# A decoder step on one core: cached keys in three passes of the rounded format, values of all sequences in one accumulator

## The chip, the core and the metric

The kernel runs on one NeuronCore of a Trainium2 chip. The metric is the device time of one execution in microseconds (us). The engines are TensorE (PE, with PEld for its weight loads), VectorE (DVE), ScalarE (ACT), GpSimd (POOL) and SyncE (SP), which only issues DMAs here.

## What is computed

One inference step of a two-layer hybrid decoder, for a prompt of 256 tokens and, at the same time, for 8 sample sequences of one new token each. Each sample sequence has 2048 past tokens in 16 pages of 128, and a page holds 256 latents and 32 rotary values a token. The change is in the attention of the 8 sample sequences over these pages (all in fp32):

```python
latent = concatenate([past_latent, latent_new])                    # S x 256
k_nope = einsum('bsc,chd->bshd', latent, w_uk)                     # 4 heads x 64
v = einsum('bsc,chd->bshd', latent, w_uv)
k = concatenate([k_nope, krope for each head])                     # 96 wide
k = _rmsnorm(k, g_qk_k)                                            # over the 96
k = concatenate([k[..., :64], _rope(k[..., 64:], pos_k)])
p = softmax(q @ k * 96 ** -0.5); o = p @ v
```

Around it, per layer: projections, a gated linear attention, pooling, the prompt's own attention, cross-attention to 256 memory rows and an MLP of 4096.

## The kernel before

Every engine has one hand-written program; semaphores connect them, and each engine runs its instructions in order. SIGNALS lists the semaphores, and `Counts` counts on each engine how often one was used. There is no planner: the order of the code is the order of the queues.

Activations lie transposed (features on partitions, 264 token columns: 256 of the prompt, 8 samples). Weights stream through `ring` (4 slots of 128x2048, SP). Weight products run in three passes of the rounded fp32 format (fp32r): ScalarE copies an operand to its rounded high part, VectorE subtracts that and rounds the rest, and TensorE adds high x high, high x low and low x high (`split_product`, L1461). Other products are fp32 (`product`, L1470), which the profile shows as two records each.

**The decode stage.** After the input projection, each layer handles its 8 sequences in 8 pairs of pages each, 64 pairs. For a pair:

- SP loads the 256 latents of both pages, transposed, into `latT` (L321). The tile holds 16 pages. A pair's place is free when TensorE is done with it (`pair_ready`), so SP runs eight pairs ahead.
- TensorE (`pair`, L1717) multiplies each page with `wuq_b`, 260 columns: 256 of `w_uk`, and 4 query columns of this sequence with the key weights folded in. That gives every cached key and its raw scores, in two PSUM banks out of four. It waits for the square and the scores two pairs before (`pair_sq`, `pair_sc`).
- ScalarE squares the 256 columns (into one of three `psq`) and copies the scores (`keys`, L578).
- VectorE sums the squares by head (`pair`, L1099, the instruction at L1102), for the norm.

Between pairs each engine has its share of the prompt's attention and of the gated linear attention: `fill(b, n)`, 41 parts at places given by PLACES; VectorE takes a part one pair later than TensorE, ScalarE two. Also between pairs, the previous sequence goes on: `rotary` (TensorE, n = 0), `scores` (VectorE, n = 0), inverse root on ScalarE, `maxima` (n = 1), a reduction over the partitions on GpSimd (L425), `exponents` (n = 2), the exponentials on ScalarE (n = 3, into `pr`), `sums` (VectorE, n = 4), and `values` (n = 5). `values` on TensorE (L1729) waits for `dec_sum`, and multiplies the 16 pages of `lat` (loaded by GpSimd, 288 values a token, L374) with `pr[:, pg, :]`, 32 columns of which four are in use, four pages at a time in the four column groups. L1738 adds the new token, L1740 the sums for the denominator. VectorE divides (L1142, L1143) into `o4`, and `latents` (L1758) adds the four groups with `sel` at the end of the next `rotary`; VectorE copies the result to `olat` (L1111).

```python
for pg in range(PAGES):
    q = 32 * (pg % 4)
    mm(t[q:q + 32, 0:256], pr[:, pg, :], lat[:, b % 2, pg, 0:256], start=pg < 4, stop=pg >= PAGES - 3)
```

During sequence 7, ScalarE and VectorE also round the memory tokens and the first weights of the stage after it. Ahead of sequence 0, VectorE prepares queries and gates (its last instruction before the first sum of squares is L953); GpSimd runs the pooling additions (L403 to L418) until about 96 us. TensorE starts pair 0 as soon as the queries of sequence 0 stand in `wuq_b` (`seq_in`).

## Time and profile before

| | us |
|---|---|
| median of 3 timed runs (lowest, highest) | 1282.72 (1279.86, 1284.19) |
| the profiled execution | 1277.03 |
| its span | 1275.4 |
| busy: TensorE, VectorE, ScalarE, GpSimd | 1220.0, 804.4, 509.6, 200.6 |
| mean granted TensorE clock | 0.983 |
| DMA | 250.42 MB, 196 GB/s |

Times in the trace are counted from the start of the span. An engine's busy time is a share of the whole span, over stages with different limits. In a row of groups, the busy time of the group is followed by the mean duration of one instruction in ns; matmuls follow each other sooner than they last, since they are pipelined. In a timeline a row merges like instructions that follow each other, and brackets give the idle time before and what ended it.

### The profile page before, as it was taken

To read this page: it belongs to the slowest core of one execution; us is meant where nothing else is said; L and a number is where in the kernel's file an instruction comes from. 1 tells how busy PE (TensorE), PEld (TensorE's weight loads), DVE (VectorE), ACT (ScalarE), POOL (GpSimd) and SP (SyncE) were. 2 spreads that over 40 slices of the span, in tenths; PEclk is the share of its full clock that TensorE was granted. 3 is DMA by queue.
4 is the path that set the end of the run, shared out by engine and by line. 5 is a ranking of instruction groups with operands and counts; after the bars stand their busy time and mean duration, and the time that the engine had idled before them with its cause. 6 is when DMAs were issued, how large, how long until landed. Compare 5 with 4: busy or idle time off the path is not lost.

```text
span 1275.4 us, 24330 instructions
## 1 busy us (share of the span) xinstructions
PE 1220.0 (96%) x9392; PEld 1101.0 (86%) x9392; DVE 804.4 (63%) x1372; ACT 509.6 (40%) x908; POOL 200.6 (16%) x343
## 2 busy tenths in 40 slices
PE   4999999989999899999999999999899999999998
PEld 4987867779988799999999777677799968999998
DVE  5568675767674776655456857646767567766442
ACT  4232322443443456543442324232443425656331
POOL 1243442220000000000012723224100000000000
PEclk9999999998999999999999999999999999999999
DMA  8615665572459744545475556447446794554552
GB/s 336 247 51 167 193 187 159 171 262 100 165 219 382 281 176 168 194 172 189 173 254 199 147 165 200 141 141 233 173 157 231 293 380 154 177 187 171 193 174 92
DMA packets 76626, 250.42 MB, mean 196 GB/s; under 512 B 11440, under 2 KB 46592, under 8 KB 55904
## 3 DMA queue, kind: packets, MB, share of 16 engines
q1 hardware_dynamic: 60976, 196.14, 43.5%
q0 software_dynamic: 13424, 45.47, 10.8%
q10 hardware_dynamic: 2112, 7.26, 1.4%
q8 instruction: 75, 1.23, 0.4%
q14 instruction: 39, 0.32, 0.1%
HBM read 241.60 MB, written 7.46 MB: 195 GB/s over the span
## 4 chain that ended last, share of the span: by engine, by line
PE 79%; DVE 7%; DMA 5%; issue 4%; ACT 2%; PEld 1%; POOLq 0%; POOL 0%; DVEq 0%; ACTq 0%; PEldq 0%
PE ps L1461 50%; PE ps L1470 19%; PE ps L1737 2%; DMA ring<-in_units 2%; DMA big<-in_pages 2%; DVE ring_r L766 1%; PE ps L1897 1%; PEld ps L1461 1%; DVE ssn L1102 1%; DVE xg_r L782 1%; DMA xT<-in_xt 1%; PE ps L1696 1%; PE ps L1697 1%; ACT big_r L454 1%; DVE rB L789 1%
## 5 line engine op out<-in xcount | busy, mean ns | idle before, releaser
L1461 PE MATMUL ps<-qkA_r,ring_r 128*128 128x264 f32 x880 | 251.9, 286 | 0.0
L1470 PE MATMUL ps<-wuq_b,latT 128*128 128x260 f32 x1024 | 249.6, 395 | 0.9 <-ACT sc L454 0.9
L1470 PEld LDWEIGHTS ps<-wuq_b,latT 128*128 128x128 f32 x1024 | 193.6, 194 | 40.8 <-issue 9.2
L374 POOL DMA_DIRECT2D big<-in_pages x256 | 138.9, 543 | 226.8 <-DVEq L730 196.8
L1461 PEld LDWEIGHTS ps<-qkA_r,ring_r 128*128 128x128 f32 x880 | 168.0, 191 | 0.0
L1461 PE MATMUL ps<-big_r,ring_r 128*128 128x264 f32 x512 | 145.5, 284 | 0.0
L766 DVE TENSOR_TENSOR ring_r<-ring,latT_r 128x2048 fp32r<-128x2048 f32 x42 | 96.3, 2292 | 61.2 <-ACT latT_r L454 60.3
L454 ACT ACTIVATE latT_r<-ring 128x2048 fp32r<-128x2048 f32 x42 | 80.4, 1915 | 111.7 <-DMA ring<-in_units 111.7
L454 ACT ACTIVATE qkA<-ps 128x512 f32<-128x512 f32 x86 | 51.1, 594 | 173.7 <-PE ps L1470 163.7
L1461 PE MATMUL ps<-xg_r,latT_r 128*128 128x264 f32 (+1 forms) x384 | 110.5, 288 | 0.0
L1461 PE MATMUL ps<-qkA_r,latT_r 128*128 128x264 f32 x320 | 94.4, 295 | 15.4 <-DVE xg_r L782 15.1
L1102 DVE TENSOR_REDUCE ssn<-qkA 128x8 f32<-128x512 f32 x86 | 59.0, 686 | 73.5 <-ACT qkA L454 69.3
L1461 PE MATMUL ps<-area_r,latT_r 128*128 128x264 f32 (+1 forms) x352 | 100.3, 285 | 0.0
L1461 PEld LDWEIGHTS ps<-big_r,ring_r 128*128 128x128 f32 x512 | 96.2, 188 | 0.0
L766 DVE TENSOR_TENSOR ring_r<-ring,big_r 128x2048 fp32r<-128x2048 f32 x28 | 67.5, 2410 | 15.2 <-ACT big_r L454 13.4
L1461 PEld LDWEIGHTS ps<-qkA_r,latT_r 128*128 128x128 f32 x320 | 61.8, 193 | 16.7 <-DVE ring_r L766 14.3
L1461 PEld LDWEIGHTS ps<-xg_r,latT_r 128*128 128x128 f32 x384 | 73.9, 192 | 0.4 <-issue 0.2
L1461 PE MATMUL ps<-qkB_r,ring_r 128*128 128x264 f32 x256 | 72.9, 285 | 0.0
L1461 PE MATMUL ps<-big_r,latT_r 128*128 128x264 f32 x256 | 72.3, 282 | 0.0
L454 ACT ACTIVATE big_r<-ring 128x2048 fp32r<-128x2048 f32 x28 | 53.1, 1910 | 47.9 <-DMA ring<-in_units 47.9
L1461 PEld LDWEIGHTS ps<-area_r,latT_r 128*128 128x128 f32 x352 | 66.2, 188 | 0.1
L766 DVE TENSOR_TENSOR ring_r<-ring,sq_r 128x2048 fp32r<-128x2048 f32 x20 | 45.8, 2291 | 31.9 <-ACT sq_r L454 31.6
(372 smaller groups left out, 2919.2 us busy)
## 6 DMA issues: line engine op xcount, KB each, us to landing
ring<-in_units SPq DMA_DIRECT2D x136, 1024.0 KB, 4.9
big<-in_pages POOLq DMA_DIRECT2D x256, 144.0 KB, 3.4
latT<-in_pages SPq DMA_DIRECT2D x256, 128.0 KB, 2.7
big<-in_units SPq DMA_DIRECT2D x12, 1024.0 KB, 10.5
mat<-in_mats POOLq DMA_DIRECT2D x2, 2048.0 KB, 11.3
mat<-in_units SPq DMA_DIRECT2D x4, 1024.0 KB, 8.4
xg<-in_memt SPq DMA_DIRECT2D x2, 1024.0 KB, 5.8
out_mk<-latT ACTq DMA_DIRECT2D x2, 1024.0 KB, 3.9
```

Of the source, the lines that this page charges most:

```text
L374: pool.dma_start(lat[:, s, pg, :], pages[bass.ds(at_page[pg] * DEPTH + l, 1), :, 256:544] .rearrange("a p n -> p (a n)")).then_inc(lat_in[ ...
L454: return nc.scalar.activation(out, in_, func, **kw)
L766: v.tensor_tensor(ring_r[:, s, :], ring[:, s, :], his[s].bitcast(FP32), ALU.subtract).then_inc(sems["unit_lo"], 1)
L782: v.scalar_tensor_tensor(xg_r[:, k, :], xT[:, k, :], gain[:, g + k:g + k + 1], hi_x[:, k, :].bitcast(FP32), ALU.mult, ALU.subtract).then_i ...
L789: step(v.tensor_tensor(rB[:, :], x_sqs[0] if k == 1 else rB[:, :], x_sqs[k % 4], ALU.add))
L1102: v.tensor_reduce(ssn[:, s, 2 * n:2 * n + 2, :], psq[(at["pair_sq"].n - 1) % 3].rearrange("p (g c) -> p g c", c=64), AXX, ALU.add).then_in ...
L1461: ins = mm(out, a(i, k), b(j, k), start=first and k + n == 0, stop=last and k == KD - 1 and n == 2)
L1470: ins = mm(out, a, b, start=i == 0, stop=i == len(pairs) - 1)
L1696: mm(t[:, c0:c0 + keys_to], normed[n_rows, i, q0:q0 + P], normed[n_rows, 4 + i, 0:keys_to], start=True, stop=False)
L1697: ins = mm(t[:, c0:c0 + keys_to], normed[r_rows, 2, q0:q0 + P], normed[r_rows, 3, 0:keys_to], start=False, stop=True)
L1737: mm(t[q:q + 32, 0:256], pr[:, pg, :], lat[:, b % 2, pg, 0:256], start=pg < 4, stop=pg >= PAGES - 3)
L1897: ins = mm(t[32 * h:32 * h + 32, 0:NM], hot[:, c, b * H + h, :], u[:, h, c, :], start=b + c == 0, stop=b + c == B)
```

## The change

**Keys.** `latT` becomes five slots of raw pairs (`raw_of`, pages 0 to 9) and three slots of high parts (`high_of`, pages 10 to 15). ScalarE writes the high part of pair n + 3 right behind the square and the scores of pair n (`key_high`); VectorE writes the low part over the raw page right behind the sum of pair n (`key_low`). Both do pairs 0 to 2 ahead of the loop. The weights and queries in `wuq_r` have both parts too. TensorE waits for `key_lo` instead of the page and runs six rounded products a page in place of two in fp32. For odd sequences the query columns stand behind the weights, for even ones ahead of them, so the weights are stored once. SP can run five pairs ahead.

**Values.** `pr` becomes 60 columns wide with one sequence's probabilities in the middle. Each sequence takes another window of 32 columns of it, so its four columns fall on other output rows, and VectorE adds the results of all sequences in one `o4` (copy, six additions, one addition with the division). The new tokens (`p_new`), the denominators and `sel` (now 32 columns) come once, with the last sequence. `values` on TensorE waits for `dec_exp` instead of `dec_sum`.

The diff, without declarations and calls that only pass a sequence's number:

```diff
@@ -24,2 +24,4 @@
 S_PAGES = PAGES + 1
+PR0 = (B - 1) * H
+WIDE_PR = PR0 + B * H
 NM = 256
...
@@ -110,2 +112,14 @@
+RAW, HIGH = 5, 3
+PAIRS = B * PAGES // 2
+def raw_of(q):
+    return slice(2 * (q % RAW), 2 * (q % RAW) + 2)
+def high_of(q):
+    return slice(2 * (RAW + q % HIGH), 2 * (RAW + q % HIGH) + 2)
 POOL_STEPS = 20
@@ -147,3 +161,2 @@
 big, big_r = twin("big", [P, 2 * PAGES * 288])
-krQ = sb("krQ", [P, PAGES, ROPE])
 krN = sb("krN", [P, PAGES, ROPE])
@@ -152,3 +165,3 @@
 rBm = sb("rBm", [P, NM + 2])
-wuq_b = sb("wuq_b", [P, 2, 2, 260])
+_, wuq_r = twin("wuq", [P, 2, 2, 264])
 qt = sb("qt", [P, 2, B, H])
@@ -161,8 +174,9 @@
 scw = sb("scw", [P, S_PAGES, H])
-pr = sb("pr", [P, S_PAGES, 32])
+pr = sb("pr", [P, PAGES, WIDE_PR])
 mxp = sb("mxp", [P, H])
 mx = sb("mx", [P, H])
-rs = sb("rs", [P, 32])
+p_new = sb("p_new", [P, B * H])
+rs = sb("rs", [P, B * H])
 den = sb("den", [P, 1])
-sel = sb("sel", [P, H])
+sel = sb("sel", [P, B * H])
 olat = sb("olat", [P, 2, B, H])
@@ -209,3 +223,4 @@
-o4 = within(qkB_f, 1024, 2, 256)
+o4 = within(qkB_f, 1024, 256)
+krQ = within(qkA_f, 1216, PAGES, ROPE)
 ssm = tmp[:, 512:512 + NM]
...
@@ -317,2 +332,3 @@
             for pg in range(PAGES):
+                q = l * PAIRS + (b * PAGES + pg) // 2
                 src = pages[bass.ds(at_page[pg] * DEPTH + l, 1), :, :].rearrange("a p n -> p (a n)")
@@ -320,3 +336,3 @@
                     sp.wait_ge(sems["pair_ready"], at["pair_ready"].free())
-                sp.dma_start(latT[:, pg, :], src[:, 0:256]).then_inc(lt_in[pg // 4], 16)
+                sp.dma_start(latT[:, raw_of(q).start + pg % 2, :], src[:, 0:256]).then_inc(lt_in[q % RAW], 16)
                 if b == B - 1 and pg == 7:
...
@@ -577,4 +592,12 @@
+        def key_high(n):
+            if n < PAIRS:
+                q = l * PAIRS + n
+                act.wait_ge(lt_in[q % RAW], 32 * (q // RAW + 1))
+                f(latT_r[:, high_of(q), :], latT[:, raw_of(q), :], ACT.Copy).then_inc(sems["key_hi"], 1)
         def keys(b, mem=False):
+            sums, scores = (slice(4, 260), slice(0, 4)) if b % 2 == 0 else (slice(0, 256), slice(256, 260))
             for pair in range(PAGES // 2):
@@ -583,5 +606,6 @@
                 q = pair % 2
-                f(psq[(at["pair_sum"].n - 1) % 3].rearrange("p (g c) -> p g c", g=2), ps[:, 4 + 2 * q:6 + 2 * q, 0:256],
+                f(psq[(at["pair_sum"].n - 1) % 3].rearrange("p (g c) -> p g c", g=2), ps[:, 4 + 2 * q:6 + 2 * q, sums],
                   ACT.Square).then_inc(sems["pair_sq"], 1)
-                f(sc[:, b % 2, 2 * pair:2 * pair + 2, :], ps[:, 4 + 2 * q:6 + 2 * q, 256:260], ACT.Copy).then_inc(sems["pair_sc"], 1)
+                f(sc[:, b % 2, 2 * pair:2 * pair + 2, :], ps[:, 4 + 2 * q:6 + 2 * q, scores], ACT.Copy).then_inc(sems["pair_sc"], 1)
+                key_high(b * (PAGES // 2) + pair + HIGH)
                 if b and pair == 1:
...
@@ -618,6 +642,9 @@
-        def exp():
+        def exp(b):
             act.wait_ge(sems["dec_in"], at["dec_in"].next())
-            f(pr[:, :, 0:H], scw[:, :, :], ACT.Exp, scale=QK ** -0.5).then_inc(sems["dec_exp"], 1)
+            f(p_new[:, H * b:H * b + H], scw[:, PAGES, :], ACT.Exp, scale=QK ** -0.5)
+            f(pr[:, :, PR0:PR0 + H], scw[:, 0:PAGES, :], ACT.Exp, scale=QK ** -0.5).then_inc(sems["dec_exp"], 1)
+        for n in range(HIGH):
+            key_high(n)
         for b in range(B):
...
@@ -857,3 +884,5 @@
-            step(v.tensor_copy(wuq_b[:, b % 2, :, 256:260], qt[:, :, b, :]))
+            c = 0 if b % 2 == 0 else 260
+            step(v.tensor_copy(wuq_r[:, 0, :, c:c + 4], qt[:, :, b, :]))
+            step(v.tensor_tensor(wuq_r[:, 1, :, c:c + 4], qt[:, :, b, :], wuq_r[:, 0, :, c:c + 4].bitcast(FP32), ALU.subtract))
             tell("seq_in")
...
@@ -888,4 +917,4 @@
                 dve.wait_ge(layer_in, 64 * (l + 1))
-                for s in range(2):
-                    step(v.tensor_copy(wuq_b[:, s, :, 0:256], w_uk))
+                step(v.tensor_copy(wuq_r[:, 0, :, 4:260], w_uk))
+                step(v.tensor_tensor(wuq_r[:, 1, :, 4:260], w_uk, wuq_r[:, 0, :, 4:260].bitcast(FP32), ALU.subtract))
                 step(v.tensor_copy(s_raw[NOPE:QK, 1, :].rearrange("p (h b) -> p h b", b=B),
@@ -1098,2 +1127,10 @@
+        def key_low(n):
+            if n < PAIRS:
+                q = l * PAIRS + n
+                wait("key_hi")
+                v.tensor_tensor(latT_r[:, raw_of(q), :], latT[:, raw_of(q), :], latT_r[:, high_of(q), :].bitcast(FP32),
+                                ALU.subtract).then_inc(sems["key_lo"], 1)
         def pair(s, n):
@@ -1109,4 +1146,2 @@
             t = tile()
-            if b:
-                step(v.tensor_copy(olat[:, :, b - 1, :], t[:, 64:72].rearrange("p (c h) -> p c h", c=2)))
             mean, rows = of_decode[1], ssn[:, b % 2, :, :]
@@ -1133,5 +1168,5 @@
-        def sums():
+        def sums(b):
             wait("dec_exp")
-            step(v.tensor_reduce(rs[:, 0:H], pr[:, :, 0:H].rearrange("p g h -> p h g"), AXX, ALU.add))
+            step(v.tensor_reduce(rs[:, H * b:H * b + H], pr[:, :, PR0:PR0 + H].rearrange("p g h -> p h g"), AXX, ALU.add))
             tell("dec_sum")
@@ -1141,4 +1176,10 @@
             t = tile()
-            step(v.reciprocal(den[:, :], t[:, 256:257]))
-            freed(v.tensor_scalar(o4[:, b % 2, :], t[:, 0:256], den[:, :], None, ALU.mult))
+            if b == 0:
+                freed(v.tensor_copy(o4, t[:, 0:256]))
+            elif b < B - 1:
+                freed(v.tensor_tensor(o4, o4, t[:, 0:256], ALU.add))
+            else:
+                step(v.reciprocal(den[:, :], t[:, 256:257]))
+                freed(v.tensor_tensor(o4, o4, t[:, 0:256], ALU.add))
+                step(v.tensor_scalar(o4, o4, den[:, :], None, ALU.mult))
             tell("lat_used")
@@ -1157,2 +1198,3 @@
                 pair(s, n)
+                key_low(b * (PAGES // 2) + n + HIGH)
                 if n == 1 and b:
...
@@ -1199,2 +1241,4 @@
         last = B - 1
+        for n in range(HIGH):
+            key_low(n)
         for b in range(B):
...
@@ -1223,3 +1267,3 @@
         mem_keys(2)
-        freed(v.tensor_copy(olat[:, :, last, :], tile()[:, 0:8].rearrange("p (c h) -> p c h", c=2)))
+        freed(v.tensor_copy(olat[:, :, :, :], tile()[:, 0:2 * B * H].rearrange("p (c b h) -> p c b h", c=2, b=B)))
         tell("olat_ready")
@@ -1500,3 +1544,3 @@
     pe.sem_inc(sems["unit_used"], SLOTS)
-    pe.sem_inc(sems["pair_ready"], PAGES // 2)
+    pe.sem_inc(sems["pair_ready"], RAW)
     for l in range(DEPTH):
@@ -1721,7 +1765,10 @@
             pe.wait_ge(sems["pair_sc"], at["pair_sc"].free())
-            if n % 2 == 0:
-                pe.wait_ge(lt_in[n // 2], 64 * (l * B + b + 1))
-            for pg in (2 * n, 2 * n + 1):
-                ins = product(ps[:, 4 + 2 * q + pg % 2, 0:260],
-                              [(latT[:, pg, P * c:P * c + P], wuq_b[:, b % 2, c, :]) for c in range(2)])
+            wait("key_lo")
+            at_pair = l * PAIRS + b * (PAGES // 2) + n
+            w0 = 4 * (b % 2)
+            for a in range(2):
+                hi, lo = (latT_r[:, of(at_pair).start + a, :] for of in (high_of, raw_of))
+                ins = product(ps[:, 4 + 2 * q + a, 0:260],
+                              [(x[:, P * c:P * c + P], wuq_r[:, j, c, w0:w0 + 260]) for c in range(2)
+                               for x, j in ((hi, 0), (hi, 1), (lo, 0))])
             ins.then_inc(sems["pair_ready"], 1)
@@ -1730,3 +1777,3 @@
-            wait("dec_sum")
+            wait("dec_exp")
             pe.wait_ge(lat_in[b % 2], 16 * PAGES * (l * (B // 2) + b // 2 + 1))
@@ -1736,6 +1783,11 @@
                 q = 32 * (pg % 4)
-                mm(t[q:q + 32, 0:256], pr[:, pg, :], lat[:, b % 2, pg, 0:256], start=pg < 4, stop=pg >= PAGES - 3)
-            mm(t[0:32, 0:256], pr[:, PAGES, :], latn[:, :], start=False, stop=True)
-            for q in range(0, P, 32):
-                ins = mm(t[q:q + 32, 256:257], rs[:, :], ones[:, 0:1], start=True, stop=True)
+                ins = mm(t[q:q + 32, 0:256], pr[:, pg, PR0 - H * b:PR0 - H * b + B * H], lat[:, b % 2, pg, 0:256],
+                         start=pg < 4, stop=pg >= PAGES - 4 + (b == B - 1))
+            if b == B - 1:
+                mm(t[0:32, 0:256], p_new[0:B, :], latn[0:B, :], start=False, stop=True)
+                pe.wait_ge(sems["dec_sum"], B * (l + 1))
+                for q in range(0, P, 32):
+                    mm(t[q:q + 32, 256:257], rs[:, :], ones[:, 0:1], start=True, stop=False)
+                    ins = mm(t[q:q + 32, 256:257], p_new[0:B, :], ones[0:B, 0:1], start=False, stop=True)
             ready(ins)
@@ -1749,11 +1801,9 @@
                 ins = product(t[:, 16 * g:16 * g + 16], [(krC[:, g, :], qbs[:, b % 2, 0:16]), (krS[:, g, :], qbs[:, b % 2, 16:32])])
-            if b:
-                ins = latents(t, 64, b - 1)
             ready(ins)
-        def latents(t, o, b):
+        def latents(t):
-            wait("lat_used")
+            pe.wait_ge(sems["lat_used"], at["lat_used"].next(B))
             for c in range(2):
-                ins = mm(t[:, o + H * c:o + H * c + H], o4[:, b % 2, P * c:P * c + P], sel[:, :], start=True, stop=True)
+                ins = mm(t[:, B * H * c:B * H * c + B * H], o4[:, P * c:P * c + P], sel[:, :], start=True, stop=True)
             return ins
...
```

VectorE's queue at the start of the stage, before the change. `ssn` is the sum of squares, `area<-ps` (L984) belongs to a fill part:

```order
L951 TENSOR_TENSOR sq<-area,sq 128x256 [waits gate_exp,tile_free]
L952 SCALAR_TENSOR_TENSOR sq<-area,sq 128x256 [waits dve_step]
L953 TENSOR_TENSOR sq<-area,sq 128x256 [waits dve_step]
L1102 TENSOR_REDUCE ssn<-qkA 128x8 [waits dve_step,pair_sq]
L1102 TENSOR_REDUCE ssn<-qkA 128x8 [waits pair_sq]
L984 TENSOR_SCALAR area<-ps 128x256 [waits tile_ready]
```

The same place in the changed kernel:

```order
L980 TENSOR_TENSOR sq<-area,sq 128x256 [waits gate_exp,tile_free]
L981 SCALAR_TENSOR_TENSOR sq<-area,sq 128x256 [waits dve_step]
L982 TENSOR_TENSOR sq<-area,sq 128x256 [waits dve_step]
L1133 TENSOR_TENSOR latT_r<-latT,latT_r 128x512 [waits dve_step,key_hi]
L1133 TENSOR_TENSOR latT_r<-latT,latT_r 128x512 [waits key_hi] x2
L1139 TENSOR_REDUCE ssn<-qkA 128x8 [waits pair_sq]
L1133 TENSOR_TENSOR latT_r<-latT,latT_r 128x512 [waits key_hi]
L1139 TENSOR_REDUCE ssn<-qkA 128x8 [waits pair_sq]
L1133 TENSOR_TENSOR latT_r<-latT,latT_r 128x512 [waits key_hi]
L1013 TENSOR_SCALAR area<-ps 128x256 [waits tile_ready]
```

Three low parts stand behind the preparation and ahead of the first sum, and one more behind each sum.

TensorE's queue in sequence 1, pairs 0 and 1, before the change (the second and fourth rows of products are fill parts):

```order
L1470 MATMUL ps<-wuq_b,latT 128x260 [waits pair_sc,pair_sq]
L1470 MATMUL ps<-wuq_b,latT 128x260 x3
L1627 MATMUL ps<-area,mat 64x256 [waits tile_free,lat_ready]
L1627 MATMUL ps<-area,mat 64x256 x11
L1470 MATMUL ps<-wuq_b,latT 128x260 [waits lt_in1,pair_sc,pair_sq]
L1470 MATMUL ps<-wuq_b,latT 128x260 x3
L1648 MATMUL ps<-area,mat 32x256 [waits tile_free]
```

And now:

```order
L1514 MATMUL ps<-wuq_r,latT_r 128x260 [waits key_lo,pair_sc,pair_sq]
L1514 MATMUL ps<-wuq_r,latT_r 128x260 x11
L1671 MATMUL ps<-area,mat 64x256 [waits tile_free,lat_ready]
L1671 MATMUL ps<-area,mat 64x256 x11
L1514 MATMUL ps<-wuq_r,latT_r 128x260 [waits key_lo,pair_sc,pair_sq]
L1514 MATMUL ps<-wuq_r,latT_r 128x260 x11
L1692 MATMUL ps<-area,mat 32x256 [waits tile_free]
```

Twelve products stand for four, and every pair waits for VectorE's low part.

## Rows read from the trace of the kernel before

**Rows 1.** The page, part 1: busy us (share of the span) xinstructions by engine.
```profile
PE 1220.0 (96%) x9392; PEld 1101.0 (86%) x9392; DVE 804.4 (63%) x1372; ACT 509.6 (40%) x908; POOL 200.6 (16%) x343
```

**Rows 2.** The page, part 5: the cached keys' products on TensorE, two records a product.
```profile
L1470 PE MATMUL ps<-wuq_b,latT 128*128 128x260 f32 x1024 | 249.6, 395 | 0.9 <-ACT sc L454 0.9
```

**Rows 3.** Busy us by stretch: PE, PEld, DVE, ACT, POOL, PEclk, DMA share, GB/s.
```profile
85.20:96.27 11.07, 11.07 (x59) 9.02 (x58) 8.38 (x14) 7.15 (x18) 9.19 (x11) 1.00 0.36 97
96.27:107.48 11.21, 11.21 (x56) 8.54 (x55) 10.42 (x18) 2.00 (x6) 8.18 (x15) 1.00 0.81 233
107.48:265.25 157.77, 152.39 (x1023) 117.66 (x1022) 101.37 (x225) 49.45 (x149) 50.92 (x96) 0.98 0.59 179
265.25:294.29 29.04, 23.94 (x159) 20.55 (x159) 21.41 (x47) 15.73 (x35) 4.32 (x9) 0.91 0.49 191
```

**Rows 4.** Who waited, 107 to 265: us in total, times, longest; VectorE and TensorE.
```profile
DVE ssn L1102 <- ACT qkA L454: 26.3, 18, 2.9
...
DVE ssn L1102 <- ACT qkB L454: 11.9, 8, 5.3
...
DVE scw L1131 <- POOL mx L425: 4.3, 2, 3.4
...
PE ps L1737 <- DVEq L730: 3.8, 3, 1.9
```

**Rows 5.** Timeline, TensorE: start us, us, engine, line, operation, count; four pairs without fills.
```profile
266.57 7.26 PE L1470 MATMUL ps<-wuq_b,latT 128*128 128x260 f32 x32
```

**Rows 6.** Busy us by stretch: rounded products without a gap, columns as Rows 3.
```profile
500.00:525.00 25.00, 25.00 (x207) 25.00 (x206) 16.89 (x23) 13.58 (x20) 0.00 (x0) 1.00 0.53 190
```

**Rows 7.** Groups of instructions, TensorE: busy us, mean ns, idle before.
```profile
L1738 PE MATMUL ps<-latn,pr 128*32 128x256 f32 x32 | 10.4, 411 | 0.0
...
L1758 PE MATMUL ps<-sel,qkB 128*128 128x4 f32 x64 | 9.2, 250 | 0.0
```

**Rows 8.** Groups of instructions on VectorE and ScalarE, same columns.
```profile
L1069 DVE TENSOR_TENSOR ring<-ring 128x512 f32<-128x512 f32 x2 | 1.4, 692 | 0.1
...
L858 DVE COPY wuq_b<-qt 128x8 f32<-128x8 f32 x16 | 2.7, 172 | 2.1
...
L454 ACT ACTIVATE krN<-big 128x512 f32<-128x512 f32 x16 | 10.0, 626 | 9.2 <-DMA big<-in_pages 9.2
```

**Rows 9.** Timeline, VectorE: two instructions without a wait between them.
```profile
206.81 0.69 DVE L1102 TENSOR_REDUCE ssn<-qkB 128x8 f32<-128x512 f32 x1
207.41 0.68 DVE L1195 TENSOR_REDUCE ssr<-krQ 128x16 f32<-128x512 f32 x1
```

**Rows 10.** Timelines of the stage's start: TensorE, VectorE, GpSimd.
```profile
78.42 3.18 PE L1470 MATMUL ps<-wuq_b,latT 128*128 128x260 f32 x8
81.44 2.32 PE L1470 MATMUL ps<-xg,ones 128*128 128x256 f32 x10
...
82.41 0.43 DVE L951 TENSOR_TENSOR sq<-area,sq 128x256 f32<-128x256 f32 x1
82.87 1.62 DVE L952 SCALAR_TENSOR_TENSOR sq<-area,sq 128x256 f32<-128x256 f32 x1
84.53 0.52 DVE L953 TENSOR_TENSOR sq<-area,sq 128x256 f32<-128x256 f32 x1
...
82.59 1.62 POOL L403 TENSOR_TENSOR area<-ue 128x798 f32<-128x798 f32 x1 [0.53 <-POOL ue L401]
...
87.36 0.69 DVE L1102 TENSOR_REDUCE ssn<-qkA 128x8 f32<-128x512 f32 x1 [1.47 <-ACT qkA L454]
...
93.11 3.12 DVE L993 TENSOR_SCALAR qsb<-area,con 128x8 f32<-128x8 f32 x4
```

**Rows 11.** Timeline, GpSimd: the first reduction over the partitions in layer 0.
```profile
118.85 0.39 POOL L425 PARTITION_ALL_REDUCE mx<-mxp  x1 [10.71 <-issue]
```

**Rows 12.** The page, part 6: pages of keys, KB each, median us to landing.
```profile
latT<-in_pages SPq DMA_DIRECT2D x256, 128.0 KB, 2.7
```

**Rows 13.** Busy us by stretch, columns as Rows 3: TensorE mostly idle.
```profile
276.00:280.00 4.00, 1.76 (x16) 1.02 (x18) 1.75 (x5) 3.16 (x8) 0.00 (x0) 1.00 0.99 414
```

19 lines of the change are left out of this document (9 added, 10 removed).

## The prediction

> **What bounds the kernel now.** I read the page's shares first: TensorE is busy for 96% of the span, VectorE for 63% [rows 1]. The costliest line but one is the product of the cached keys: 1024 records, 249.6 us, with 0.9 us of waiting before them [rows 2]. Then the busy times by stretch. In layer 0 the decode stage goes from VectorE's first sum of squares at 85.20 to its last at 294.29, 209.1 us. In sequences 1 to 6 (107.48 to 265.25) TensorE is busy for 152.4 of 157.8 us, VectorE for 101.4 [rows 3]. What VectorE waits for there is ScalarE's squares, 26.3 + 11.9 us [rows 4], and these come from TensorE's products. So TensorE sets the pace of the stage, and VectorE has a third of it free. No instruction outside this stage is edited to speak of, and layer 1 has the same program as layer 0: I work out one layer and double it.
>
> **What TensorE saves.** Four pairs with nothing between them took 7.26 us: 1.8 us a pair [rows 5]. Products in the rounded format run at 25 us / 207 = 0.121 us each for 264 columns at the full clock [rows 6]; a pair now has 12 of them, 1.45 us. That is 0.35 x 128 = 45 us. L1738, the new token's latents, goes in 14 of 16 sequences at 10.4 / 16 = 0.65 us, L1758 falls from 64 records to 4, 9.2 us to 0.6 [rows 7]: 9 + 9 us. Together 63 us, if TensorE kept the pace. It does not.
>
> **What VectorE gets.** Each of 64 pairs a layer adds one TENSOR_TENSOR of 128x512, 0.69 us [rows 8]. No wait for its own step stands behind it, and an instruction after such a one starts 0.60 us later (206.81, 207.41) [rows 9]; I take 0.60. Where an instruction does wait for the step before, 0.035 us pass in between (82.41 + 0.43, next at 82.87) [rows 10]. The other edits on VectorE (a small one more for the queries, a reciprocal and a copy gone, an addition for a multiplication) cancel: nothing. So per layer [rows 3]:
> - Sequences 1 to 6: 101.4 busy, 225 gaps x 0.035 = 7.9, 48 x 0.60 = 28.8: 138.1 us, where 157.8 passed: **-19.7**. TensorE's own work there is 152.4 - 48 x 0.35 - 6 x 1.2 = 128: VectorE is the bound now.
> - Sequence 7: 21.4 + 1.6 + 5 x 0.60 = 26.0, where 29.0 passed: **-3.0**.
> - Sequence 0 from pair 4 on: 10.4 + 0.6 + 4 x 0.60 = 13.4, where 11.2 passed: **+2.2**. VectorE sets the pace there already.
>
> ScalarE gets one copy of 128x512 a pair, 0.63 us by the copy to krN [rows 8]: 40 us beside its 67 in these three stretches of 198 us. It stands right behind the square and the scores of the same pair, while VectorE sums that square for 0.69 us. I count nothing.
>
> **The start of the stage.** TensorE began pair 0 at 78.42, beside VectorE's preparation, whose last instruction (L953) ended at 85.05. Now pair 0 waits for key_low(0), which stands behind that preparation in VectorE's queue and is reached at about 85.6. GpSimd's additions run there (busy for 9.2 of the next 11.1 us, [rows 3]): in the shadow of one, from 82.59, VectorE's L952 took 1.62 us, where L951 of the same size took 0.43 [rows 10]. Held as long, key_low(0) ends at 87.4. TensorE has idled for nearly 9 us by then and comes back at the half clock, as it ran pair 0 in the trace, 3.18 us for eight records: 2.9 us for 12 rounded products at twice 0.121. Then fill part 0 (2.3 us at full clock, I take 2.6), pair 1 and ScalarE's square: VectorE sums pair 1 at 95.0, not at 87.36. Its work from there to pair 4 was 8.4 - 0.7 = 7.7 us busy; with gaps and three key_lows 10.0. But the four instructions L993, 3.12 us for 128x8, ran beside GpSimd and would come after it now, where 128x8 takes some 0.2 (L858): -2.2 [rows 8, 10]. Pair 4 is reached at 102.8 instead of 96.27: **+6.5**. Bounds: +4 (nothing held, full clock), +9 (no -2.2).
>
> **The waits that stay.** Where VectorE is the bound, each wait of its own is paid. One is sure: the first reduction over the partitions in a layer comes late, with 10.7 us on GpSimd that nothing in the view explains, and VectorE waited 3.4 us for it [rows 4, 11]. A key_low now stands ahead of it: 2.8. For the rest there are two ends. From 96.27 to 107.48, where VectorE sets the pace, 0.2 of 11.2 us was waiting, 2%; over all of sequence 0 it was 22.3 less 18.8 and 1.1 of gaps, 11%. On the 164 us above that is 3.3 or 18 us; I take 7.7, nearer the first, because TensorE may run three pairs ahead and has over 30 us to spare. This is to cover the heavy fills, pages that land late, and the later reductions, which stand behind sixteen page loads in GpSimd's queue. In all **+10.5**.
>
> Five slots for raw pairs instead of eight cost nothing in the forecast: a slot comes free about two pairs (6 us) before ScalarE wants its next content, and a page lands after 2.7 us [rows 12]. Without that cover each pair would cost up to a microsecond; the upper end has it.
>
> **Sum.** -19.7 - 3.0 + 2.2 + 6.5 + 10.5 = -3.5 us a layer, -7 in all: 1277.0 becomes 1270.0 for the profiled execution. The median of the timed runs is 5.7 us above that execution, so the forecast is **1275.7 us**, 0.5% faster. Under 0.3%, 3.9 us, a measurement of this kernel hardly tells from no change.
>
> **A rule against the change.** In the 4 us from 276, TensorE was busy for 1.76 and its clock was still the full one, 1.00 [rows 13]. VectorE as the bound gives TensorE gaps of half a microsecond a pair, far less idle time than that, so the sum counts its work at the full clock. The Trainium skill (TensorE: Matmul & The Clock Gate, HAM oscillation) says that waits between bursts of matmuls bring the throttle back again and again. By that rule the sum would be that of rival 2; the trace does not bear it out for such a short idle time.
>
> **Rivals.**
> 1. *VectorE keeps its waits; slower.* The place is the hand-over in sequences 1 to 6: a key_low holds VectorE's fill part behind it, and TensorE's products wait for the key_low of three pairs before. If the engines take turns instead of overlapping, VectorE keeps, say, 60% of its 42.5 us of waiting there [rows 4] and of 6 in sequence 7: 29 instead of 10.5, which is +15 a layer, +30 in all, 1313. It decides from 14 us of waits a layer, where the gain is gone; above 16 the kernel is slower by over 0.3%. For it: TensorE waited 3.8 us there for VectorE's sums of the exponents already [rows 4]. Against it: the values' product no longer waits for these.
> 2. *TensorE at the half clock for half of the stage; slower.* Its work of some 199 - 32 = 167 us a layer, less 4 for the low clock already in it, becomes 163 / 0.75 = 217, more than VectorE's. With the start at +6.5 that is 15 us a layer more than the 209 now: 1313. For it: pair 0 above ran at the lower clock after small products. Against: [rows 13].
> 3. *The waits almost vanish.* Only the reduction and the 2% stay, 6.2 us: -8 a layer, 1267; with the start at +4, 1262. For it: TensorE's reserve.
> 4. *TensorE stays the bound and all of its 63 us show*: 1220. VectorE's sum excludes it, unless the added instruction costs far less than 0.60. It would be the change as its TensorE part alone reads.
>
> **Numbers.** By waits of 7 to 14 us a layer the forecast goes from 1269 to 1283: 0.50. Rival 1, above 14 us, up to 1313: 0.26. Rival 2: 0.06. Rival 3, below 7 us: 0.16. Rival 4: 0.02. From 1259 to 1302 leaves out rivals 2 and 4, a third of rival 1 and a little of rival 3: two in ten. Faster by over 0.3% (under 1278.9, up to 12 us of waits) are rivals 3 and 4 and two thirds of the forecast: 0.52; within it 0.19; slower (over 1286.5) 0.29.
>
> **What would show it.** Right: 1.45 us a pair for the keys on TensorE; VectorE busy for over 85% in sequences 1 to 6, its waits for ScalarE's squares under 10 us there, and TensorE waiting for key_low instead; TensorE idle for 8 to 9 us before pair 0; a stage of some 206 us. Wrong: a TensorE still without gaps, a key_low that takes its place at another price than 0.60, or a VectorE busy for under 80% of the stage.

## The result and the profile after

The changed kernel took 1313.86 us (median of 4 runs, 1306.78 to 1318.06), the kernel before 1283.45 (4 runs): a ratio of 1.0235, 95% interval 1.0178 to 1.0291. It is **slower** by 30 us; the forecast was 1275.7 with a range from 1259 to 1302. The profiled execution took 1306.78 us, with a span of 1305.0; the one of before had a span of 1275.4.

The page of after, parts 1 (busy time, share, instructions) and 2 (three of its rows):

```profile
PE 1198.2 (92%) x9724; PEld 1105.5 (85%) x9724; DVE 883.3 (68%) x1490; ACT 576.6 (44%) x1052; POOL 202.8 (16%) x342
...
PE   4978989889999899999999698898699999999998
...
DVE  5569788778674677664556888978757657766432
...
PEclk8979899888999999999999799989899999999999
```

Beside [rows 1], TensorE is busy for 22 us less and VectorE for 79 us more. The two decode stages are slices 3 to 10 and 23 to 29, and there the granted clock now dips. Over the span it is 0.954, before it was 0.983.

The page, part 5, the two costliest groups of the change:

```profile
L1514 PE MATMUL ps<-wuq_r,latT_r 128*128 128x260 f32 x1536 | 227.4, 304 | 40.1 <-DVE latT_r L1133 29.9
...
L1133 DVE TENSOR_TENSOR latT_r<-latT,latT_r 128x512 fp32r<-128x512 f32 x128 | 93.1, 730 | 0.3
```

The first answers [rows 2]. The keys' products take 22 us less, not 45, and TensorE has idled 40 us before them, mostly for VectorE's split, where it idled 0.9.

The stretches of layer 0 that answer to [rows 3] (from the first sum of squares to pair 4 of sequence 0, to sequence 1, sequences 1 to 6, sequence 7), and a last row for all of them in layer 1; the columns are those of [rows 3]:

```profile
92.35:105.65 13.30, 13.30 (x96) 12.21 (x95) 10.73 (x18) 10.00 (x25) 9.94 (x14) 0.95 0.49 141
105.65:119.27 13.62, 10.62 (x73) 8.76 (x71) 12.84 (x21) 3.92 (x10) 4.10 (x8) 1.00 0.67 225
119.27:277.68 158.41, 143.34 (x1125) 118.59 (x1125) 128.96 (x269) 74.18 (x203) 48.63 (x92) 0.91 0.54 167
277.68:309.16 31.48, 26.50 (x173) 23.35 (x173) 24.01 (x50) 17.92 (x40) 6.11 (x12) 0.73 0.63 226
732.30:946.75 214.45, 185.09 (x1454) 154.53 (x1454) 173.83 (x349) 105.11 (x274) 68.30 (x124) 0.93 0.57 179
```

The stage of layer 0 ends at 309.16 and not at 294.29, 14.9 us later (its last sum of squares starts at 306.16, before at 291.25); the whole span grew by 29.6. Layer 1's last sum starts 27.5 us later than before, so nearly the whole loss lies in these stages. Sequences 1 to 6, where the forecast had its gain, take 158.4 us, as long as before. VectorE's busy time there rose from 101.4 to 129.0, and the granted clock there is 0.91 where it was 0.98.

Who waited in these sequences, 119 to 278 (us in total, times, longest), VectorE's waits and TensorE's largest:

```profile
DVE ssn L1139 <- ACT qkB L469: 7.8, 4, 4.0
...
DVE ssn L1139 <- ACT qkA L469: 6.2, 6, 1.8
PE ps L1514 <- DVE latT_r L1133: 4.9, 3, 2.8
...
DVE scw L1166 <- POOL mx L440: 2.8, 1, 2.8
```

VectorE's waits for squares fell from 38.2 us [rows 4] to 14.0, and TensorE now waits for the low halves. Both engines wait, in turn: neither is the bound of the whole stretch. Of the 29.9 us that TensorE waited for the low halves, 18.2 are the two waits ahead of pair 0, one a layer; in sequences 1 to 6 it was 4.9 in layer 0 and 3.9 in layer 1.

The start of the stage, timelines of TensorE and VectorE (start, duration, engine, line, operation; in brackets the idle time ahead):

```profile
88.75 2.94 PE L1514 MATMUL ps<-wuq_r,latT_r 128*128 128x260 f32 x12 [9.18 <-DVE latT_r L1133]
...
86.84 3.17 DVE L1133 TENSOR_TENSOR latT_r<-latT,latT_r 128x512 fp32r<-128x512 f32 x3
92.35 0.69 DVE L1139 TENSOR_REDUCE ssn<-qkA 128x8 f32<-128x512 f32 x1 [2.34 <-ACT qkA L469]
92.95 1.88 DVE L1133 TENSOR_TENSOR latT_r<-latT,latT_r 128x512 fp32r<-128x512 f32 x1
```

TensorE stands for 9.2 us before pair 0 and takes 2.94 us for its 12 products, at the level of 1.2 GHz. At 2.4 GHz, 24 of them took 3.15 us (101.42), 1.5 to 1.6 a pair. Of the splits, the first took 1.77 us, the fourth 1.88 and the fifth 1.43, while GpSimd added beside them; of 128, the mean is 0.73.

### The profile page after: what moved, and what is told of

Its sections match the earlier page's. It is cut to its first block, busy times and chain, and to the rows that moved or that the text cites. A ratio compares the mean times of both kernels' runs of the same rounds, so it can differ in the third digit from the quotient of the medians.

```text
span 1305.0 us, 25249 instructions
## 1 busy us (share of the span) xinstructions
PE 1198.2 (92%) x9724; PEld 1105.5 (85%) x9724; DVE 883.3 (68%) x1490; ACT 576.6 (44%) x1052; POOL 202.8 (16%) x342
## 4 chain that ended last, share of the span: by engine, by line
PE 64%; DVE 20%; issue 6%; DMA 4%; ACT 3%; PEld 1%; POOL 0%; POOLq 0%; DVEq 0%; ACTq 0%; PEldq 0%
PE ps L1505 49%; PE ps L1514 9%; DVE latT_r L1133 3%; DVE ssn L1139 3%; DMA ring<-in_units 2%; DMA big<-in_pages 2%; DVE ring_r L793 2%; PE ps L1947 1%; PEld ps L1505 1%; DVE xg_r L809 1%; DVE qkB L1226 1%; PE ps L1740 1%; DMA xT<-in_xt 1%; DVE qkB L1225 1%; PE ps L1741 1%
## 5 line engine op out<-in xcount | busy, mean ns | idle before, releaser
L1514 PE MATMUL ps<-wuq_r,latT_r 128*128 128x260 f32 x1536 | 227.4, 304 | 40.1 <-DVE latT_r L1133 29.9
L1514 PEld LDWEIGHTS ps<-wuq_r,latT_r 128*128 128x128 f32 x1536 | 206.6, 203 | 61.4 <-issue 46.1
L1133 DVE TENSOR_TENSOR latT_r<-latT,latT_r 128x512 fp32r<-128x512 f32 x128 | 93.1, 730 | 0.3
L469 ACT ACTIVATE latT_r<-latT 128x512 fp32r<-128x512 f32 x128 | 80.7, 634 | 1.1 <-DMA latT<-in_pages 1.1
```

What stands on the lines that cost most here:

```text
L469: return nc.scalar.activation(out, in_, func, **kw)
L1133: v.tensor_tensor(latT_r[:, raw_of(q), :], latT[:, raw_of(q), :], latT_r[:, high_of(q), :].bitcast(FP32), ALU.subtract).then_inc(sems["key ...
L1514: ins = mm(out, a, b, start=i == 0, stop=i == len(pairs) - 1)
```

## The experiments

Eleven kernels ran, each timed against the kernel before on the same chip. They ran on three chips, on which the kernel before took 1282.0, 1282.8 and 1279.2 us: where two of them differ by a few us, the ratios to it say more than the times. All end in one table, at the end of this section. The expectations speak of theories by letters; each is spelled out where it first stands.

### The two parts of the change alone

**The values' part.** The accumulator of all sequences is kept; pages, weights and products of the keys are those of before:

```diff
-                    wait("key_lo")
...
-                                       for x, j in ((hi, 0), (hi, 1), (lo, 0))])
+                    if n % 2 == 0:
+                        pe.wait_ge(lt_in[n // 2], 64 * (l * B + b + 1))
...
+                                      [(latT[:, pg, P * c:P * c + P], wuq_b[:, b % 2, c, :]) for c in range(2)])
```

Expected: 

> The values of all sequences in one accumulator, with the keys in fp32 as before. The change came out 30 us slower than before, and the question is where. Theory V (VectorE has become the bound of sequences 1 to 6 and hands over late, since the split pages gave it 128 more instructions of 0.73 us): this part takes nothing to VectorE, so it gains what TensorE saves in it, at most the 18 us of [rows 7], 1265 to 1275 us. Theory C (TensorE waits more and runs at its 1.2 GHz level after it): also faster, 1265 to 1278, and the windows at 1.2 GHz in the decode stage are as few as before. Theory A (the one accumulator itself costs, by the chain of additions into o4 or the values' wait): 1290 or more.

Measured: 1265.82 us (ratio 0.987, 0.9843 to 0.9898). This part alone is **faster by 16 us** and is the fastest kernel here that leaves nothing out of the computation.

**The keys' part.** The reverse: three rounded passes, with a sum, a division and a turn for each sequence as before.

```diff
-                    if b == 0:
-                        freed(v.tensor_copy(o4, t[:, 0:256]))
...
+                    step(v.reciprocal(den[:, :], t[:, 256:257]))
+                    freed(v.tensor_scalar(o4[:, b % 2, :], t[:, 0:256], den[:, :], None, ALU.mult))
```

Expected: 

> The keys in three rounded passes with split pages, with the values as before (a sum and a division for each sequence). Theories V and C: the whole loss lies here, so 1314 plus what the values' part saves, 1320 to 1332 us. Theory A: nearly as fast as before, 1275 to 1290 us.

Measured: 1319.7 us (1.0287, 1.0254 to 1.0319). The whole loss is the keys' part: 37 us alone. Theory A falls. The two parts do not add up: +37 and -16 would give +21, and both together cost +30. Beside the keys' part the values' part is worth 6 us (1319.7 to 1313.9), not 16. It saves TensorE's time, and where TensorE waits for others anyway, less of that shows.

### What the keys' part costs on VectorE

**Without the split.** The high part is taken a third time in the place of the low one, so the low half of the cached keys is left out of the computation:

```diff
-                        wait("key_hi")
-                        v.tensor_tensor(latT_r[:, raw_of(q), :], latT[:, raw_of(q), :], latT_r[:, high_of(q), :].bitcast(FP32),
-                                        ALU.subtract).then_inc(sems["key_lo"], 1)
...
-                    wait("key_lo")
+                    wait("key_hi")
...
-                        hi, lo = (latT_r[:, of(at_pair).start + a, :] for of in (high_of, raw_of))
+                        hi, lo = (latT_r[:, of(at_pair).start + a, :] for of in (high_of, high_of))
```

Expected: 

> The changed kernel without VectorE's split: the third pass takes the high part again in the place of the low part, so TensorE has the same 12 products a pair and ScalarE the same copies, and VectorE has none of its 128 subtractions (the low half of the cached keys is left out of the computation). Theory V: VectorE's 93 us are off the path, the decode stage is TensorE's again at 1.45 us a pair, 20 to 30 us a layer less than in the change: 1255 to 1275 us. Theory C (the clock level falls of itself in a stage of short rounded passes, whoever is waited for): the windows at 1.2 GHz stay as many, and the time is 1285 to 1305. Theory S (ScalarE's copies of the pages delay its squares, not VectorE's split): 1295 or more.

Measured: 1261.64 us (0.9864, 0.9826 to 0.9901), 52 us under the change. TensorE and ScalarE have the same instructions. VectorE was busy for 803.9 us and not 883.3 (the group's 93 us count overlaps between neighbours twice): 79 us of its work cost 52 us of time. Theory C as stated there falls, and so does S. Theory V has the time right; that the stage is TensorE's again is refuted below, by the run with two passes. The 52 us are not the price of VectorE's work alone: this kernel also loses the hand-over through VectorE ahead of each pair, and with it the late start. Of the 55 us between the two profiled executions, some 24 lie ahead of sequence 1 (12.25 in layer 0, 107.02 against 119.27).

**The reverse.** To the values' part alone, with its fp32 keys, one VectorE instruction of 128x512 a pair is added:

```diff
+                        step(v.tensor_reduce(idle[:, :], con[:, 0:512].rearrange("p (g c) -> p g c", g=8), AXX, ALU.add))
```

Expected: 

> The values' part alone (1265.8 us, keys in fp32) with one more VectorE instruction of 128x512 a pair that nobody reads, 128 of about 0.69 us, 88 us in all, in the place where the split stands. Theory V1 (TensorE's fp32 keys leave VectorE room: the split's VectorE work costs something only because the keys' own time shrinks beside it): 1265 to 1275 us. Theory V2 (VectorE's hand-overs are on the path before the change too, so its added work costs as it stands): 1285 to 1310 us.

Measured: 1309.0 us (1.0205, 1.0142 to 1.0268), 43 us more; VectorE's busy time is 84 us more. Theory V1 falls. Nobody waits for the added instruction, so this is the price of a fuller VectorE queue alone. Even where TensorE's fp32 keys leave VectorE idle for a third of sequences 1 to 6, half of what is added to VectorE is paid over the whole kernel. By place the price differs: in sequences 1 to 6, 33 us of added work a layer cost 8 us in layer 0 and 12 in layer 1; from pair 4 of sequence 0 on, 2.7 cost 2.9; in sequence 7, 4.8 cost 6.7 in layer 0 and 3.7 in layer 1.

**The same on ScalarE**, a copy of 128x512 a pair.

```diff
+                        step(f(idle[:, :], con[:, 0:512], ACT.Copy))
```

Expected: 

> The values' part alone (1265.8 us) with one more ScalarE copy of 128x512 a pair that nobody reads, 128 of 0.4 to 0.65 us, in the place where the copy of the high part stands. The counterpart of the 88 us of VectorE work, which cost 43 us. Theory S0 (ScalarE, busy for 40% of the time, has the room, as the prediction took it): 1263 to 1271 us. Theory S1 (ScalarE's squares and exponents are on the hand-overs' path, so each copy ahead of them costs in part): 1275 to 1300.

Measured: 1268.91 us (0.992, 0.9889 to 0.9951; 10 runs), 3 us more for 70 us of work by the medians, 6 by the ratios. Counting nothing for ScalarE was right, nearly.

Sequences 1 to 6 of layer 0 in five kernels, columns as in [rows 3]. The values' part alone:

```profile
106.99:259.31 152.32, 149.80 (x944) 113.23 (x942) 99.34 (x215) 50.16 (x155) 50.38 (x95) 0.97 0.60 183
```

The same with VectorE's added work:

```profile
111.69:272.00 160.31, 148.21 (x939) 110.52 (x938) 132.02 (x262) 50.00 (x155) 48.65 (x92) 0.98 0.56 168
```

The high part three times:

```profile
107.02:252.31 145.29, 134.33 (x1133) 110.95 (x1132) 100.67 (x220) 73.98 (x203) 50.17 (x95) 0.97 0.60 184
```

The high part in two passes (below):

```profile
107.49:251.67 144.18, 124.07 (x950) 96.60 (x949) 100.66 (x221) 73.76 (x203) 48.35 (x92) 0.88 0.60 182
```

The early split with products to fill (below):

```profile
114.84:271.88 157.04, 148.97 (x1266) 127.39 (x1266) 128.96 (x269) 75.00 (x203) 48.50 (x92) 0.98 0.56 169
```

Read the first number beside VectorE's, the third. In these five, with 99 to 101 us of VectorE work the stretch takes 144 to 152 us; with 129 to 132 it takes 157 to 160. TensorE's work goes from 124 to 150 in the first class and changes the time of the stretch by 8. VectorE's work is not all of it, though: the kernel before, with 101.4, took 157.8 us [rows 3], where TensorE was busy for 152.4, and the keys' part alone, with 131.2, took 166.7, where TensorE waited 11.7 us ahead of the values' products, which still wait for VectorE's sums there:

```profile
PE ps L1777 <- DVEq L754: 11.7, 6, 3.3
```

In the second class the clock of 0.98 in the last row, against 0.91 in the change, goes with 1.4 us less; at 0.86, in the early split's profile, the same stretch took 165.4.

The same sequences in layer 1: before, the values' part alone, the high part three times, the change.

```profile
731.81:891.75 159.94, 154.39 (x1024) 118.52 (x1022) 101.46 (x226) 49.63 (x149) 51.82 (x98) 0.97 0.58 176
728.14:880.41 152.27, 149.88 (x945) 113.31 (x943) 99.34 (x214) 50.17 (x155) 50.67 (x96) 0.97 0.60 184
718.55:863.84 145.29, 133.78 (x1134) 110.26 (x1132) 100.69 (x221) 74.00 (x203) 50.01 (x95) 0.98 0.59 184
758.59:916.27 157.68, 140.57 (x1125) 115.20 (x1125) 129.30 (x268) 74.83 (x203) 48.90 (x92) 0.94 0.55 167
```

That gives the balance of this stretch, each step one kernel, layer 0 and in brackets layer 1: before 157.8 us (159.9); the values' part takes 5.5 off (7.7); the rounded products another 7.0 (7.0), to 145.3 (145.3); VectorE's split, with TensorE's wait for it, puts 13.1 back (12.4), to 158.4 (157.7). What TensorE saved was real, and the split took all or nearly all of it back. These are single profiled executions.

### Whether TensorE's time is still wanted

**Two passes** in the place of three, on the kernel without the split: the high half of the pages against both halves of the weights, 8 products a pair.

```diff
-                                       for x, j in ((hi, 0), (hi, 1), (lo, 0))])
+                                       for x, j in ((hi, 0), (hi, 1))])
```

Expected: 

> The kernel of the run with the high part three times (1261.6 us, no split on VectorE) with two passes in the place of three: 8 products a pair and not 12, 512 fewer, some 0.12 us each at full clock, 62 us of TensorE's work (the low half of the cached keys stays left out). Theory T (with VectorE unburdened, TensorE's products are the path again): 1205 to 1235 us. Theory W (TensorE's saved time in the stage mostly turns into waiting for VectorE's sums and ScalarE's squares, and into stretches at 1.2 GHz): span times granted clock 10 to 30 lower than 1224, the clock below 0.965, 1235 to 1258 us.

Measured: 1262.51 us (0.9876, 0.9814 to 0.9938), against 1261.64: **62 us of TensorE's work removed, nothing gained**. Theory T falls. W named both what happened and missed the size: span times clock is 34 us lower, where it allowed 30, while the clock fell to between 0.937 and 0.945 and the time stayed. Sequences 1 to 6 of layer 0 took 144.2 us against 145.3, at a clock of 0.88 against 0.97. Whether the lower clock took the gain, or the hand-overs would have kept the stretch as long at any clock, these two runs do not separate. TensorE's and VectorE's waits in sequences 1 to 6 of this kernel:

```profile
DVE ssn L1137 <- ACT qkA L469: 13.0, 11, 3.0
PE ps L1821 <- ACT qkA L469: 12.8, 5, 4.3
DVE ssn L1137 <- ACT qkB L469: 12.2, 4, 5.4
...
DVE scw L1164 <- POOL mx L440: 5.1, 3, 3.5
```

VectorE still waits for 30 us here, though TensorE has 20 us of its own to spare. These waits stand at the hand-overs of the stage (square, sum, rotary keys, maxima, exponents), and they stayed with room on both engines.

### The clock

**Filling the idle time before pair 0.** 64 products that nobody reads, ahead of the first pair of a layer, in the changed kernel:

```diff
+                wait("seq_in")
+                for _ in range(64):
+                    mm(ps[:, 7, 264:512], wuq_r[:, 0, 0, 4:132], wuq_r[:, 0, 1, 4:252])
```

Expected: 

> The changed kernel; TensorE takes 64 products of 248 columns with an unused result while it waits for the first split of a layer (9.2 us idle in the change, at the level of 1.2 GHz after it: the first 12 products took 2.94 us). Theory C (the idle time costs the clock, and the clock is the larger part of the loss): the stretch at 1.2 GHz behind pair 0 goes, although nothing starts earlier; 2 to 8 us less a layer, 1298 to 1309 us, granted clock up by 0.003 to 0.006. Theory L (only the late start costs): no change, 1311 to 1317 us. If the 64 products take longer than the wait, the time grows: 1316 to 1322.

Measured: 1301.29 us (1.0166, 1.0108 to 1.0225), **12.6 us less by adding work**, by the medians, at clocks of 0.957 to 0.966 (the change: 0.945 to 0.956). The size is less sure than the sign: by the ratios it is 9 us, the two intervals overlap a little (1.0178 to 1.0291 for the change), and the two profiled executions are 7.8 us apart. The timeline of TensorE:

```profile
78.03 8.73 PE L1840 MATMUL ps<-wuq_r 128*128 128x248 f32 x64
87.10 1.69 PE L1514 MATMUL ps<-wuq_r,latT_r 128*128 128x260 f32 x12 [0.35 <-DVE latT_r L1133]
```

Pair 0's products take 1.69 us, not 2.94, and pair 4's sum comes at 101.92, not 105.65. Of these 3.7 us, 1.65 are that pair 0 starts earlier, since the products of the stage ahead ended at about 78.0 and not at 79.6 in this execution; the rest is mostly the clock. By the end of the stage it is 6.4 us. Theory L, that only the late start costs, falls; C holds, with a clock up by some 0.01 where it said 0.003 to 0.006.

**Filling at each pair**, on the kernel with the early split (next):

```diff
+                    for _ in range(3):
+                        mm(ps[:, 4 + 2 * q, 0:248], wuq_r[:, 0, 0, 4:132], wuq_r[:, 0, 1, 4:252])
                     wait("key_lo")
```

Expected: 

> The kernel with the early split (1293.6 us at clocks of 0.954 to 0.968) and three products more of 248 columns ahead of each pair's products, with an unused result: 384 products, 0.36 us a pair at full clock, 46 us of work for TensorE in all. Theory C: they lie where TensorE waits in any case, keep it at 2.4 GHz, and so cost less than a third of their time: clock 0.975 or more, 1285 to 1305 us. Theory T (TensorE is short of time in this stage, whatever its clock): 1320 to 1340 us. A stage that is VectorE's for its work alone, with the clock of no account, gives 1293 to 1300 at an unchanged clock.

Measured: 1299.93 us (1.0129, 1.0077 to 1.0181), 6.4 more than without, which is not clear of the spread (1.0088, 1.0059 to 1.0118 without), at clocks of 0.975 to 0.977 (0.954 to 0.968 without). Theory C said less than a third of 46 us and a clock of 0.975, and has both; T falls. The last case has the time right and the clock wrong. The products keep the clock up, and yet the time does not fall. So the clock alone does not explain the 30 us: with it nearly back at the level of before, this kernel is still 17 us slower than before.

### Where the instructions stand

**The early split**: the first three low halves right behind the first queries, ahead of 6 us of VectorE's preparation.

```diff
                 key_queries(0)
                 key_queries(1)
+                for n in range(HIGH):
+                    key_low(n)
...
-                for n in range(HIGH):
-                    key_low(n)
```

Expected: 

> The changed kernel with the first three VectorE splits moved up its queue, from behind all of its preparation to right behind the first two sequences' queries. Theory L (the late start of the stage, the 9.2 us in which TensorE stands before pair 0, is the larger part of the loss): pair 0 starts near 82 instead of 88.75 us, the first sum 4 to 7 us earlier, the clock stays up, and the time is 8 to 14 us less over two layers, 1300 to 1306. Theory V: VectorE still has its 6 us of preparation before the first sum; pair 0 comes early but the stage's end moves by 0 to 3 us a layer, 1308 to 1314.

Measured: 1293.57 us (1.0088, 1.0059 to 1.0118; 5 runs), 20 us less than the change, more than either theory gave. In the profile pair 0 starts at 79.09 and pair 4's sum at 100.20, 5.5 us earlier than in the change. The late start of the forecast is thus real; that it is worth all 20 us is not shown, since only 2 of them are less span times clock and the rest goes with the clock (0.954 to 0.968).

**Only pair 0's split early.**

```diff
-                for n in range(HIGH):
-                    key_low(n)
+                key_low(0)
...
+                key_low(1)
+                key_low(2)
                 for b in range(B):
```

Expected: 

> The kernel with the early split, but only pair 0's split ahead of VectorE's preparation, and those of pairs 1 and 2 behind it again. Moving all three took 20 us from the time, though it let TensorE wait again behind pair 0 (4.9 us in one profile), for the decay products that VectorE prepares. Theory L (the start is the cause of what is left): the first sum 1 to 3 us earlier, 1286 to 1291 us. Theory V (the walls of sequences 1 to 7 are VectorE's and stay): 1290 to 1296.

Measured: 1297.9 us (1.015, 1.0095 to 1.0206). No better: TensorE idles for 4.9 us behind pair 0 in this profile, and for 3.6 behind pair 1, not behind pair 0, in that of the early split. Sequences 1 to 6 take 158.3 us there, as in the change.

**The split last in each step**, on both engines, behind all that hands over.

```diff
                         pair(s, n)
-                        key_low(b * (PAGES // 2) + n + HIGH)
...
                         elif n == 7 and mem and l == 0:
                             newton(P, NM + 2, rBm[:, :])
+                        key_low(b * (PAGES // 2) + n + HIGH)
```

Expected: 

> The kernel with the early split; in each step VectorE's and ScalarE's split instructions stand behind what hands over to other engines (maxima, exponents, rotary keys) in the place of ahead of it. Theory H (the split pages, done three pairs ahead, delay what is due at once; 0.7 us of VectorE and 0.6 us of ScalarE each time): 4 to 12 us less, 1282 to 1290 us. Theory V (VectorE's sum of work bounds, in whatever order): within 3 us, 1290 to 1297. If three pairs ahead is too short once the split comes later: 1300 or more, with TensorE waiting for key_low more often.

Measured: 1297.35 us (1.0119, 1.0057 to 1.0181). Theory H falls: this order brings nothing that shows. It isn't free of effects, though. In sequences 1 to 6 of layer 0 TensorE now waited 12.5 us for the low halves, in 10 waits, against 3.8 in 2 with the early split alone, which is what the third case expected of a split that comes late. A gain on the hand-overs could hide behind that.

### All runs

Each execution has its span and its mean granted clock. Their product, in the third column, is nearly the same for all executions of one kernel, while the time moves with the clock: 28 of the kernel before went from 1276 to 1290 us and held 1251 to 1260.

```
kernel                          median us   span x clock   clock
before                          1279-1283   1251-1260      0.974-0.988
the change                      1313.9      1244-1251      0.945-0.956
values' part alone              1265.8      1240-1243      0.978-0.986
keys' part alone                1319.7      1252-1261      0.951-0.960
early split                     1293.6      1240-1253      0.954-0.968
high part three times           1261.6      1221-1229      0.966-0.983
fill before pair 0              1301.3      1244-1254      0.957-0.966
early split, fill at each pair  1299.9      1263-1268      0.975-0.977
early split, split last         1297.4      1248-1252      0.961-0.968
values + VectorE work           1309.0      1266-1272      0.965-0.974
high part in two passes         1262.5      1189-1191      0.937-0.945
values + ScalarE work           1268.9      1241-1246      0.975-0.985
one split early                 1297.9      1237-1247      0.953-0.962
```

Between before and the change the product falls by some 9 us, close to the 7 that the forecast's sum gives; the clock falls from 0.98 to 0.95, and the time grows by 30. The product is a way of counting, not a cause: it also falls when TensorE simply has less to do at an unchanged time, as with two passes. That the clock falls because TensorE waits is borne out by the two kernels with products to fill, in which it rose; that it costs time only where TensorE's products come next on the path is my reading, and no run isolates it.

## Why the prediction was wrong

By its own steps, in layer 0, where the sum said -3.5 us and the trace shows +14.9:

- **What TensorE saves.** 1.45 us a pair was near: 1.5 to 1.6 at full clock. The values' terms were right: 18 us of TensorE's work, and 16 us of time in the run of that part alone, where TensorE kept the pace.
- **What VectorE gets.** 0.60 us a split was right: 129.0 - 101.4 = 27.6 us for 48, 0.57 each. "VectorE is the bound now" was right as far as its work decides, but its busy share in sequences 1 to 6 is 81%, not over 85, and its waits for squares are 14.0 us there, not under 10.
- **Sequence 0 from pair 4 on**: +2.4 (forecast +2.2).
- **The start**: pair 4's sum stands at 105.65, 9.4 us later, of which 1.3 came from the stage ahead (the products ahead of it start at 76.59, before at 75.29): 8.1 against 6.5, within its bounds. The 9 us of idle time, pair 0 at 2.9 us and L993's gain were as told. What was missed is that GpSimd held more than the first of the splits: the fourth and the fifth took 1.88 and 1.43 us.
- **The waits that stay, +10.5: the step that failed.** Sequences 1 to 7 were to take 12.2 us less with it and took 3.1 more: without any waits the sum had them 22.7 shorter, so the waits were 25.8 us in its own terms, where it said 10.5; what the lower clock cost there is in it. In sequences 1 to 6 VectorE idled for 29.5 us: 12.1 in gaps of up to 0.3 us, of which the sum had 7.9 by 0.035 each, and 17.4 in named waits. The price of the waits came from the few steps in which VectorE was already late, and nothing in the rest of the stage was asked. But VectorE's idle time was no store to draw on. In the kernel with two passes, where neither engine is pressed, it still idles for 43.5 of 144.2 us. Its waits stand at the hand-overs, and added work in the queue can delay the next one. So VectorE's work had a price long before TensorE's share of the time was used up: 43 us for 84 by adding it where nobody waits for it, 52 for 79 by taking the split and its wait away. In sequences 1 to 6, where the sum had its gain, the split's 28 us cost 13.1 in layer 0 and 12.4 in layer 1, as much as TensorE had saved there. The sum let VectorE's work cost nothing until it filled the stretch. Which hand-over it delays most, no run took apart.
- **The clock, counted as unchanged.** The row of 4 us at 1.00 [rows 13] did not carry over, though it was read rightly: one short row was too little for a whole stage. In sequence 1 (119.27 to 149.03) TensorE was busy for 28.8 of 29.8 us, with no wait over 1.0 us in it and one of 2.0 just ahead, and its clock was 0.83. The Trainium skill (TensorE: Matmul & The Clock Gate, HAM oscillation) says that the throttle comes back between bursts of matmuls. The runs agree that waits bring it: behind the 9.2 us of waiting pair 0 ran at 0.50, and with products in that wait at 1.00. In sequence 1 the waits were short: 1.0 us at 110, 2.0 at 117 and 1.0 at 127, then products of 64 columns, and from 132 to 141 the clock was 0.50 with TensorE busy throughout. The same small products ran at 1.00 in the kernel before, from 116.35 to 122.58, with no such waits ahead of them. So there the small products alone don't bring it. The change from 132 to 141, and the kernel before from 116.35 to 122.58, columns as in [rows 3]:

```profile
132.00:141.00 9.00, 9.00 (x54) 6.92 (x57) 7.88 (x16) 3.64 (x10) 0.19 (x1) 0.50 0.18 50
116.35:122.58 6.23, 6.23 (x53) 4.77 (x52) 3.06 (x6) 2.51 (x7) 0.39 (x1) 1.00 0.27 70
```

- **ScalarE and the five slots at nothing**: ScalarE's copies are worth 3 us; in the whole stage of layer 0 it waited 1.1 us for pages of keys, so five slots were enough.
- **The rivals.** Rivals 1 and 2 both said 1313, and what happened is mostly the first; the clock of the second fell too, but to 0.91 in sequences 1 to 6, where half the stage at half the clock would be 0.75. That 1313 is met to the us is luck in part: rival 1 had 29 us of waits a layer where it was 25.8, and 6.5 at the start where it was 8.1, with 1.3 more from the stage ahead. Rival 1's place was right (hand-overs in sequences 1 to 6; the engines take turns). Its chance of 0.26 was too low because the term above had been priced from the wrong steps. How the 30 us divide between waits and clock isn't settled: filling the idle time ahead of pair 0 gives 9 to 12.6 back, of which a part is an earlier start; filling at each pair brings the clock back and no time; and with VectorE's split gone the clock recovers by itself.
- **A label.** The 294.29 that the sum calls the last sum of squares is three us behind it, where a split for the next stage starts; the last sum starts at 291.25. It changes nothing: by the last sums, too, the stage ends 14.9 us later.

## What to carry to other kernels

Idle time on an engine in a stage of many small hand-overs is not room. Before moving work to it, ask in which steps it waits and in which it is waited for, and price the added work until a run says otherwise. Here it cost a quarter to a half of its time in the middle of the stage, all of it where VectorE was nearly full already, and half over the whole kernel; a dummy instruction in the old kernel measures that in one run. When a change has two parts, run each alone; here one gained 16 us and the other lost 37, and together they lost 30. And if a change shortens TensorE's part, look at the granted clock behind each of its waits: time saved on TensorE can turn into waits at a lower clock.

## What the runs showed of the hardware

- 512 products fewer (62 us at 0.12) left the time as it was, 1262.5 against 1261.6 us; the mean granted clock fell from 0.966-0.983 to 0.937-0.945.
- 64 products that nobody reads, in a wait of 9.2 us, made the kernel 12.6 us faster by the medians (9 by the ratios to before); the 12 products after them took 1.69 us in the place of 2.94.
- The granted clock was 0.50 from 132 to 141 us of the change while TensorE was busy throughout, behind waits of 1.0, 2.0 and 1.0 us and small products; in the kernel before the same products ran at 1.00. Three products more ahead of each pair brought the kernel's mean clock from 0.954-0.968 to 0.975-0.977, and no time.
- A subtraction of 128x512 with two inputs in SBUF took 0.68 us alone and up to 1.88 beside GpSimd's additions.
- The first reduction over the partitions in a layer started late in every kernel; VectorE waited 2.8 to 3.6 us for it in layer 0 and 3.0 to 4.3 in layer 1, and the view names no cause.
